# The block sums of the down projection's weight tiles: added on chip by GpSimd, in place of accumulating transfers through DRAM

## What is computed

```python
D_MODEL = 2048; SEQ = 256; D_FF = 5632
def conv_gated_ffn(h, w_up, conv_w, conv_b, w_down):
    S = h.shape[1]
    u = h @ w_up
    up = jnp.pad(u, ((0, 0), (CONV_W - 1, 0), (0, 0)))
    c = conv_b + sum(up[:, j:j + S] * conv_w[j] for j in range(CONV_W))
    gate, val = c[..., :D_FF], c[..., D_FF:]
    return (jax.nn.silu(gate) * val) @ w_down
```

## Time and profile before

| what | value |
|---|---|
| time, median of 3 runs | 1037.89 us (1037.18 to 1038.49) |
| span of the profiled execution | 1035.4 us |
| time of the profiled execution | not listed apart; the median is 2.5 us over its span |
| PE, DVE, ACT, POOL busy | 99%, 77%, 71%, 9% |
| down projection | from about 786 us to 1029 us of the span |
| transfers from w_down into DRAM sums | 60 of 512 KB, 6.6 us to landing |
| accumulating transfers inside DRAM | 40 of 256 KB, 6.6 us to landing |
| loads in the down projection | 68 of 512 KB and 20 of 256 KB from w_down, 40 of 512 KB from the sums |

### The profile page before, as it was taken

How to read it: one execution, slowest core, us unless ns; L and a number is a source line. 1 busy time by engine, 2 the same in 40 slices (tenths; PEclk the granted TensorE clock), 3 DMA queues, 4 the chain that set the end, 5 groups by cost and what they waited for, 6 DMA issues and landing times.

```text
span 1035.4 us, 15993 instructions
## 1 busy us (share of the span) xinstructions
PE 1026.6 (99%) x5141; PEld 858.3 (83%) x5141; DVE 793.9 (77%) x1026; ACT 734.5 (71%) x1191; POOL 88.9 (9%) x150
## 2 busy tenths in 40 slices
PE   9999999999999999999999999999999999999997
PEld 8888888888888888888888888888888878888885
DVE  5679787887767578768687787876868999887677
ACT  6966474745556687988879888798887766646664
POOL 1000000000111111111111111111111000000000
PEclk9999999999999999999999999999999999999999
DMA  9676767667899999898999998989999589888993
GB/s 295 188 225 178 238 189 224 191 208 215 271 285 321 282 290 269 264 266 278 264 288 254 280 263 269 282 254 278 261 274 264 167 306 316 295 289 285 319 313 113
DMA packets 156103, 266.85 MB, mean 258 GB/s; under 512 B 11908, under 2 KB 60388, under 8 KB 155936
## 3 DMA queue, kind: packets, MB, share of 16 engines
q1 hardware_dynamic: 138224, 222.67, 65.7%
q0 software_dynamic: 17360, 43.22, 18.9%
q10 hardware_dynamic: 480, 0.47, 0.1%
HBM read 256.86 MB, written 44.06 MB: 291 GB/s over the span
## 4 chain that ended last, share of the span: by engine, by line
PE 98%; DMA 1%; SPq 0%; DVE 0%; ACT 0%; issue 0%; DVEq 0%
PE pj L1523 12%; PE pj L1528 12%; PE pj L1524 12%; PE pj L1536 9%; PE tr_ps L1528 9%; PE tr_ps L1523 9%; PE tr_ps L1524 9%; PE pj L1541 5%; PE sc_ps L1528 4%; PE sc_ps L1523 4%; PE sc_ps L1524 4%; PE pj L1558 3%; PE pj L1551 2%; PE pj L1517 1%; PE pj L1519 1%; PE pj L1518 1%
## 5 line engine op out<-in xcount | busy, mean ns | idle before, releaser
L1000 DVE TENSOR_TENSOR split<-raw,split 128x1024 fp32r<-128x1024 f32 x265 | 321.6, 1222 | 159.6 <-ACT split L641 153.8
L641 ACT ACTIVATE split<-raw 128x1024 fp32r<-128x1024 f32 x259 | 272.7, 1056 | 125.1 <-PE pj L1528 26.0
L929 ACT ACTIVATE split<-raw 128x1024 fp32r<-128x1024 f32 (+1 forms) x125 | 121.6, 989 | 63.6 <-PE sc_ps L1528 27.9
L1335 DVE TENSOR_TENSOR split<-raw,split 128x1024 fp32r<-128x1024 f32 (+1 forms) x125 | 138.2, 1136 | 31.0 <-ACT split L929 29.3
L1523 PE MATMUL tr_ps<-split,act_split 128*128 128x512 f32 x352 | 136.9, 389 | 0.0
L1524 PE MATMUL tr_ps<-split,act_split 128*128 128x512 f32 x352 | 136.9, 389 | 0.0
L1523 PE MATMUL pj<-split,act_split 128*128 128x512 f32 x352 | 136.9, 389 | 0.0
L1524 PE MATMUL pj<-split,act_split 128*128 128x512 f32 x352 | 136.9, 389 | 0.0
L1536 PE MATMUL pj<-act_split,split 128*128 128x512 f32 x416 | 131.6, 398 | 0.0
L1528 PE MATMUL tr_ps<-split,act_split 128*128 128x512 f32 x352 | 94.1, 389 | 0.0
L1528 PE MATMUL pj<-split,act_split 128*128 128x512 f32 x352 | 94.1, 389 | 0.0
(11 more groups left out here) (249 smaller groups left out, 1660.9 us busy)
## 6 DMA issues: line engine op xcount, KB each, us to landing
raw<-w_up SPq DMA_DIRECT2D x176, 512.0 KB, 5.8
raw<-w_in SPq DMA_DIRECT2D x72, 512.0 KB, 4.3
raw<-w_down SPq DMA_DIRECT2D x68, 512.0 KB, 6.0
t_dram<-w_down POOLq DMA_DIRECT2D x60, 512.0 KB, 6.6
raw<-t_dram SPq DMA_DIRECT2D x40, 512.0 KB, 6.0
raw<-w_o SPq DMA_DIRECT2D x32, 512.0 KB, 6.3
t_dram<-t_dram POOLq DMA_DIRECT2D x40, 256.0 KB, 6.6
raw<-w_down SPq DMA_DIRECT2D x20, 256.0 KB, 6.1
```

What stands on the lines that cost most here:

```text
L641: ins = act.activation(hi[:, slot, 0:TILE], raw[:, slot, 0:TILE], ACT.Copy)
L929: act.activation(hi[:, slot, c0:TILE], down_raw(t)[:, c0:TILE], ACT.Copy).then_inc(hi_done, 1)
L1000: dve.tensor_tensor(lo[:, slot, 0:n], raw[:, slot, 0:n], hi[:, slot, 0:n].bitcast(F32), ALU.subtract).then_inc(lo_done, 1)
L1335: dve.tensor_tensor(lo[:, slot, c0:TILE], down_raw(t)[:, c0:TILE], hi[:, slot, c0:TILE].bitcast(F32), ALU.subtract).then_inc(lo_done, 1)
```

## The change

Nothing is added up in DRAM any more. SP loads b1 and all of b2 of a unit into its first two raw slots and skips parts 2 and 3. GpSimd waits for both loads, and makes t13 and t42 with four additions of 128 x 512 fp32, from SBUF to SBUF, straight into the raw slots of parts 2 and 3. ACT then waits for `t13_s` and `t42_s` in place of a load. Since GpSimd reads b1 and b2, a load into a slot that held one of them also waits for the `t42_s` of that unit. The last transfer that POOL issued (`gfin`, the final norm's gain, 1 MB) moves to SP's queue, ahead of tile 76.

```diff
+def loaded(t):
+    return DOWN[t][1] == "plain" or DOWN[t][2] < 2
...
+def raw_free(t):
+    last = raw_before(t)[-1]
+    kind, part = DOWN[last][1:3]
+    return last, sums_index(last - part) + 1 if kind == "sums" and part < 2 else 0
...
             for t, (g, kind, part, kt) in enumerate(DOWN):
+                if t == GROUP_END[0] + GFIN_AFTER:
+                    sp.wait_ge(z_s, 8)
+                    sp.dma_start(gfin[:], norm_final.partition_broadcast(P)).then_inc(d_gf, 16)
+                if not loaded(t):
+                    continue
                 if t < RING:
                     sp.wait_ge(lo_done, T_DOWN + t - (RING - 1))
                 elif raw_before(t):
-                    sp.wait_ge(lo_done, T_DOWN + raw_before(t)[-1] + 1)
+                    last, sums_made = raw_free(t)
+                    sp.wait_ge(lo_done, T_DOWN + last + 1)
+                    if sums_made:
+                        sp.wait_ge(t42_s, 2 * sums_made)
...
-                elif part == 1:
-                    sp.dma_start(dst[:, 512:TILE], wdn[kt][:, 1, (2 * g + 1) * 512:(2 * g + 2) * 512]).then_inc(d_w[raw_slot(t)], 16)
-                else:
-                    j = sums_index(t - part)
-                    sp.wait_ge(tsum_s, j + 1)
-                    sp.dma_start(dst, (t13_dram, t42_dram)[part - 2][j]).then_inc(d_w[raw_slot(t)], 16)
+                half = part
+                sp.dma_start(down_raw(t)[:, 0:TILE].rearrange("p (c n) -> p c n", c=2),
+                             wdn[kt][:, :, (2 * g + half) * 512:(2 * g + half + 1) * 512]).then_inc(d_w[raw_slot(t)], 16)
...
-            def weight_sums(turn):
...
-                    pool.dma_start(t13_dram[j].rearrange("p (c n) -> p c n", c=2), w[:, :, right],
-                                   accum_op=ALU.add).then_inc(t_done[i], 16)
...
+            def weight_sums(j):
+                t = UNITS[j]
+                b1, b2 = down_raw(t), down_raw(t + 1)
+                t13, t42 = down_raw(t + 2), down_raw(t + 3)
+                left, right = slice(0, 512), slice(512, TILE)
+                for n in range(2):
+                    pool.wait_ge(d_w[raw_slot(t + n)], slot_loads(t + n))
+                for n in range(2, 4):
+                    if raw_before(t + n):
+                        pool.wait_ge(lo_done, T_DOWN + raw_before(t + n)[-1] + 1)
...
+                if j > 0:
+                    pool.wait_ge(t42_s, 2 * j)
+                pool.tensor_tensor(t13[:, left], b1[:, left], b2[:, left], ALU.add).then_inc(t13_s, 1)
+                pool.tensor_tensor(t13[:, right], b2[:, left], b2[:, right], ALU.add).then_inc(t13_s, 1)
+                pool.wait_ge(t13_s, 2 * j + 1)
+                pool.tensor_tensor(t42[:, right], b2[:, right], t13[:, left], ALU.add).then_inc(t42_s, 1)
+                pool.wait_ge(t42_s, 2 * j + 1)
+                pool.tensor_tensor(t42[:, left], b1[:, right], t42[:, right], ALU.add).then_inc(t42_s, 1)
...
-            for turn in range(TSUM_TURNS):
-                weight_sums(turn)
-
-            pool.wait_ge(z_s, 8)
-            pool.dma_start(gfin[:], norm_final.partition_broadcast(P)).then_inc(d_gf, 16)
+            for j in range(len(UNITS)):
+                weight_sums(j)
...
-                act.wait_ge(d_w[raw_slot(t)], slot_loads(t))
+                if loaded(t):
+                    act.wait_ge(d_w[raw_slot(t)], slot_loads(t))
+                else:
+                    act.wait_ge((t13_s, t42_s)[part - 2], 2 * sums_index(t - part) + 2)
```

More of the change, by code:

```diff
@@ L58 @@
 EXTRA = 2
+GFIN_AFTER = 12
 COMBINE = {0: (0,), 1: (1, 2), 2: (3,), 3: (4,)}
@@ L94, in raw_before @@
     return [s for s in range(t) if raw_slot(s) == raw_slot(t)]
+def loaded(t):
+    return DOWN[t][1] == "plain" or DOWN[t][2] < 2
 def slot_loads(t):
     slot = raw_slot(t)
[L100 to L112, removed]
+    return (T_DOWN // RING * 16 + (32 if slot % 2 == 0 else 0) if slot < RING else 0) + 16 * (sum(map(loaded, raw_before(t))) + 1)
+def raw_free(t):
+    last = raw_before(t)[-1]
+    kind, part = DOWN[last][1:3]
+    return last, sums_index(last - part) + 1 if kind == "sums" and part < 2 else 0
+UNITS = [t for t, d in enumerate(DOWN) if d[1:3] == ("sums", 0)]
 WO_ORDER = [(0, 0), (0, 1), (0, 2), (0, 4), (0, 5), (0, 6), (1, 0), (1, 1), (1, 2), (1, 4),
@@ L316, in program @@
         d_w = [sem(f"d_w{i}") for i in range(RING + EXTRA)]
-        t_done = [sem(f"t_done{i}") for i in range(2)]
-        tsum_s = sem("tsum_s")
+        t13_s, t42_s = sem("t13_s"), sem("t42_s")
         d_x = [sem(f"d_x{i}") for i in range(4)]
@@ L350, in program @@
         seeded_s = sem("seeded_s")
-        t13_dram = nc.dram_tensor("t13_dram", (TSUMS, P, TILE), F32).ap()
-        t42_dram = nc.dram_tensor("t42_dram", (TSUMS, P, TILE), F32).ap()
         nft_dram = nc.dram_tensor("nft_dram", (NH, S), F32).ap()
@@ L551, in _ @@
                 pool.wait_ge(d_x[c], 32)
[L553 to L570, removed]
@@ new lines, in weight_sums @@
+            def weight_sums(j):
[9 more added lines that the diff above has]
+                    else:
+                        pool.wait_ge(glo_s, UP_PAIRS)
+                    if raw_slot(t + n) < RING:
+                        pool.wait_ge(lo_done, T_DOWN)
+                if j > 0:
[6 more added lines that the diff above has]
+                pool.tensor_tensor(t42[:, left], b1[:, right], t42[:, right], ALU.add).then_inc(t42_s, 1)
```

4 lines of the change are left out of this document (removed).

## The result

The changed kernel takes 1106.66 us in the median of four runs (1105.19 to 1107.34), the kernel before on the same chip 1037.72 us; the ratio is 1.0659, with a 95% interval of 1.0644 to 1.0674 (the two medians alone divide to 1.0664). The forecast was 1090 us with a range of 1050 to 1130. It moved the way the prediction says and lies inside the range, 17 us over the forecast.

A forecast was written before the change was run, and what follows sets the result against it. PE was taken to bound the kernel, busy for 99% of the span. Lateness of 38.6 us in group 0 and 18.5 in group 1, less 5, gave +52 on 1035.4, span 1087; with 2.5 for the median 1090 us, range 1050 to 1130.

The forecast's parts named there:

- What bounds the kernel: Whole kernel: PE is busy for 99% of the span, so removed DRAM traffic gains about 0, at most 0.7 us.
- The loop: Down projection: b2's load, four GpSimd additions, then the next b2; one-P period 12.0 us in group 0, 10.3 in group 1.
- the eight intervals: Second to last unit of a group: six turns behind one P, two behind two P's; PE alone needs 65.4 us.
- The shared reads: Down projection: GpSimd cannot read SBUF during a two-operand DVE instruction, so their work is laid end to end; lo's add 1.9 us.
- For the loop it matters little who waits: Additions' window: whether DVE also is held up by GpSimd was left open, as their work is summed either way.
- 2.5 us of lead: Group 1's second unit: b2 issued 15 us before PE needs t42, so this lead is eaten first, leaving 18.5 us.
- 5 us of lead at the t42 of the first unit: Group 0's start: this lead against a second unit needing about 16 us to PE's 7.5; net 4 us late.
- The part taken off: All 16 intervals: an addition's fixed 0.2 us need not exclude DVE's reads; a third of a microsecond each, -5 us.
- Moved and free: SP's queue: gfin moved there stands ahead of a tile whose predecessor waits for sums anyway; about 0.
- Hidden: Rival: the loop is shorter than PE's period, up to 0.96 us an addition, so no change; 1038 us, chance 6%.
- The loop without ports: Rival: GpSimd and DVE pass each other, turns 8.4 and 10.4 us; 1047 us, up to 1058, chance 12%.
- The clock: Rival: PE's waits drop its clock towards 1.2 GHz, making PE the bound again; 1130 to 1170 us, chance 10%.

The follow-up runs named there:

- e1: Changed kernel with GpSimd writing one column in place of each addition from the third unit on, loads and waits kept: 1036.57 us, ratio 0.9987.
- e2: Changed kernel with each GpSimd addition replaced by three chained memsets that write SBUF and read nothing: 1072.67 us, ratio 1.0339.
- e4: Changed kernel with a seventh raw slot, so behind one P no load waits for the t42 of the unit before: 1091.80 us, ratio 1.0523.
- e11: Changed kernel with the four additions replaced by four one-operand copies of 128 x 512 in the same chain: 1049.83 us, ratio 1.0117.
- e3: Changed kernel with each addition covering 256 of the 512 columns from the third unit on: 1059.90 us, ratio 1.0214.
- e6: Kernel before, sums still from DRAM, plus 20 times four GpSimd additions on constant SBUF data that nobody waits for: 1088.34 us, ratio 1.0486.
- e9: Changed kernel with gfin loaded behind the last unit, ahead of tile 120: 1105.04 us, ratio 1.0647.
- e14: Kernel before with only group 1's sums made on chip, by four VectorE additions, group 0's still from DRAM: 1037.31 us, ratio 0.9993.

## Why the prediction was right, and where its sizes were off

**What bounds the kernel.** Right. PE had no idle time to win back: without the additions (e1) the time is 1036.57 us, 1 us under the kernel before. The "gain of about 0" was a gain of about 0.1%.

**The loop.** Right as a mechanism. The chain of the changed kernel shows it turn by turn, e2 has it without the reads, and e4, which cuts it behind one P, takes group 1 from 30.1 us late to 13.3.

| term | forecast | measured |
|---|---|---|
| t42 done to the next addition, one P | 4.2 us | 3.9 us (993.46 to 997.32) |
| addition of 512 columns, alone | 1.03 us | 1.26 to 1.28 us |
| four additions with the turns of lo, group 1 | 6.1 us | 7.1 us (997.32 to 1004.41) |
| turn behind one P, group 0 / group 1 | 12.0 / 10.3 us | 11.4 / 11.0 us, mean of six |
| turn behind two P's, group 0 / group 1 | 14.0 / 12.3 us | 13.3 / 12.5 us |
| the eight intervals, group 0 / group 1 | 100.0 / 86.4 us | 95.0 / 90.9 us |
| late, group 0 / group 1 | 38.6 / 18.5 us, less 5 for both | 38.0 / 30.1 us |

The addition was undersized, though the copies it was worked out from were right (e11: 0.61 us). The step "if a second operand doubles the cost of an element" was off in size: e3 and the changed kernel give 2.1 ns a column for two operands, against 0.8 ns for a copy, 2.6 times and not twice. The estimate from the Trainium skill's "GPSIMD Engine Reference", section "Performance versus the Vector engine", was 1.12 us and so nearer, but still under the 1.26 us here.

**The shared reads.** Right, and the open half of it is answered: GpSimd holds VectorE up just as well, 1.27 us for an instruction of 0.29 us. Of the Trainium skill's rule in "SBUF — State Buffer", "Who interferes with whom", the runs now show both directions, and that a GpSimd instruction that only writes is no party to it (e2: no lo over 1.23 us). Laying the two engines' work end to end gave the turn of group 0 to 0.5 us: 11.9 us were forecast, and 11.4 measured. By e4 and e6, and by the chain of group 0, it is this, and not the loop, that sets group 0. "For the loop it matters little who waits" was right for the period and hid that in group 0 the loop is only the second of two limits that lie together. The loop taken away alone (e4) leaves group 0 where it is; the reads taken away alone (e2), which also shortens the loop's turn to 9.5 us, halve its loss.

**Where each group starts.** In group 1 this is the term that was most off. I gave it 2.5 us of lead, with b2 of its second unit issued 15 us before PE needs its t42. It was issued later. Its slot waits for the t42 of the first unit, and GpSimd could begin that unit only at 959.78 us, when lo of tile 66 had freed the slot of tile 72, 8 us before PE reached the unit. So t42 was ready only at 966.9 us. The slot waits for lo of tile 69 as well, and this, held up by an addition, ended last. DVE's row of it, and SP's issue of b2:

```profile
965.71 2.30 DVE L1315 TENSOR_TENSOR split<-raw,split 128x1024 fp32r<-128x1024 f32 x1
...
968.04 0.37 SPq L528 DMA_DIRECT2D raw<-w_down  x1
```

From there to the next unit's first addition at 974.1 us it took 6.0 us, where the forecast has 4.2 for issue and load; gfin went out 0.4 us behind this load. Instead of using up a lead of 2.5 us the second unit made PE 3.5 us later (38.7 us late at its first matmul, 42.2 behind it). That is 6 of the 12 us by which group 1 is off. Another 4.5 are the eight intervals, from longer additions; the last 1 us is not traced.

In group 0 the same slip stands, and is hidden. I counted 5 us of lead at the t42 of the first unit. GpSimd's first unit there ran so:

```profile
824.30 2.03 POOL L573 TENSOR_TENSOR raw<-raw 128x512 f32<-128x512 f32 x1 [608.55 <-DVE split L1315]
...
830.86 1.62 POOL L578 TENSOR_TENSOR raw<-raw 128x512 f32<-128x512 f32 x1
```

It had to wait for lo of tile 9 (done at 824.04), whose slot its t42 takes. So t42 was ready at 832.5 us, when PE, which reached the unit at 829.4, was about to need it, and PE was 3.5 us late by the unit's last tile. The eight intervals add 95.0 - 65.4 = 29.6 us where 34.6 were forecast, so 8.4 us of group 0's lateness lie outside them, where 4 were forecast. The two errors offset each other: that 38.6 us stand against 38.0 is in part luck.

**The part taken off.** The 5 us for the fixed part of an addition, 2.5 for each group, have the right sign in group 0, where 95.0 us stand against 100.0, and the wrong one in group 1. No run tests the reason given for them.

**Moved and free.** gfin was costed at about 0. It makes one wait for a load 2 us longer, and the span of e9 is 1.2 us shorter without it, which the runs do not tell from nothing.

**The rivals.** Hidden: no. Its threshold of 0.96 us an addition fits what group 1 shows on either side, 1.2 us late with 0.73 us (e3) and 30.1 with 1.27 us, but no run lies near it. The loop without ports: e2 is this case with 1.47 us for each addition, 34 us late. The clock: it did fall in the units, and "the clock shows under 1.0 in the middle of the stage" was one of the signs by which I had called myself wrong. The mean granted clock was 0.91 from 834 to 934 us and 0.97 from 960 to 1060 us (the windows under e4). It fell eight times for a few us each, five times in group 0 and three times in group 1. PE over three stretches of group 1 of the changed kernel (us, busy, granted clock, DMA share, GB/s):

```profile
1014.00:1018.00 4.00, 2.39 (x8) 1.00 0.34 104
1018.00:1022.00 4.00, 4.00 (x12) 0.57 0.79 262
1022.00:1026.00 4.00, 4.00 (x19) 1.00 0.08 31
```

After PE had stood idle for 1.6 of 4 us, the granted clock was 0.57 in the next 4 us, so near the lower level of 1.2 GHz for most of them, and back at 2.4 GHz in the third stretch. By the Trainium skill's "TensorE: Matmul & The Clock Gate", in the section on the clock gate, an idle engine falls to 1.2 GHz. The trace agrees in that each fall comes behind waits of PE. But the turn from 1043.26 to 1054.15 us, which holds another such stretch, takes 10.9 us, as long as the one from 997.32 to 1008.23, which holds none. And TensorE is not in the chain that ended last, in either group (the shares by line above): a slower PE falls into its waits. So the sign came true without the case that it stood for, where PE would have become the bound. No run takes the clock's fall away by itself, so that its price is small is argued from this and not measured; in e2, which lacks the reads, the clock did not fall within the stage either, so what lies between e2 and the changed kernel is not free of it.

The other signs came out. PE was 0.3 us late at the first unit, its idle time grew by 41 us where about 50 were forecast, the turns are 11.4 and 11.0 us long, and an addition beside a lo takes up to 2.3 us.

## What to carry to other kernels

Before moving element-wise work to an idle GpSimd, look at what VectorE does beside it: if it reads two SBUF operands most of the time, GpSimd's reads are paid by VectorE, and here doing the four additions on VectorE itself (2.5 us) was cheaper than having GpSimd do them (3.7 us or more). Ask of each buffer that a new engine reads when it comes free, and follow the release around to that engine's next input: a ring with one slot too few turns the producer's latency, the load's and the addition's, into a period. When two limits lie within half a microsecond of each other, an experiment that removes one may show nothing, as e4 did in group 0, though that one would hold the kernel up by itself (e2); take each away alone before you rule one out.

## What the runs showed that was not expected

GpSimd and VectorE take turns instruction by instruction when both have reads waiting, so a short VectorE instruction pays most in proportion (0.29 us becomes 1.27 us). The 43 MB of software-queue traffic in DRAM, nearly a sixth of all bytes, were worth about 0.1% to a kernel bound by TensorE (e1 without them, at most 0.2% by its interval), and half of them nothing that e14 could tell.
